# A mixture-of-experts trunk in fp32: the experts' down products cut into matmuls of 256 moving columns

## What is computed

```python
def swiglu(h, w_gate, w_up, w_down):
    return (jax.nn.silu(h @ w_gate) * (h @ w_up)) @ w_down

def moe_swiglu(h, w_router, w_gate, w_up, w_down):
    logits = (h @ w_router).astype(jnp.float32)
    top_vals, top_idx = lax.top_k(logits, TOP_K)          # TOP_K = 2 of 8
    gates = jax.nn.softmax(top_vals, axis=-1)
    comb = jnp.sum(jax.nn.one_hot(top_idx, N_EXPERTS, dtype=jnp.float32) * gates[..., None], axis=-2)
    out = jnp.zeros_like(h)
    for e in range(N_EXPERTS):
        out = out + comb[..., e:e + 1].astype(h.dtype) * swiglu(h, w_gate[e], w_up[e], w_down[e])
    return out
```

## Time and profile before

| | us |
|---|---|
| median of 3 runs | 1464.48 (1464.02 to 1464.84) |
| span of the profiled execution | 1463.9 |
| TensorE busy | 1434.9 |
| VectorE busy | 1167.5 |
| ScalarE busy | 925.6 |
| DMA queue of the weights, share of 16 engines | 77.5% |

### The profile page before, as it was taken

The page is one execution under the profiler, slowest core; times in us unless marked ns, Lnnn a source line. Parts: engine busy times, 40 slices in busy tenths (PEclk is TensorE's granted clock), DMA queues, the critical chain, the costliest instruction groups (busy, mean ns, idle before and its releaser), DMA issues.

```text
span 1463.9 us, 25480 instructions
## 1 busy us (share of the span) xinstructions
PE 1434.9 (98%) x10712; PEld 1312.7 (90%) x10712; DVE 1167.5 (80%) x1101; ACT 925.6 (63%) x918; POOL 42.5 (3%) x62
## 2 busy tenths in 40 slices
PE   7999999999999999999999999999999999999996
PEld 6899999998889889999999888999999898999994
DVE  6676556568637998998988998899798889989895
ACT  3845434444516777776776767676676767767675
POOL 2030000003020000000000000000000000000000
PEclk9999999999998999999999999999999999999998
DMA  8466555553219998999999999899999989999931
GB/s 332 144 227 227 189 189 199 199 184 136 72 49 417 368 382 336 366 363 339 357 348 368 332 378 360 335 357 353 351 349 361 367 342 354 357 350 360 355 146 45
DMA packets 60001, 426.14 MB, mean 291 GB/s; under 512 B 7025, under 2 KB 7153, under 8 KB 8689
## 3 DMA queue, kind: packets, MB, share of 16 engines
q1 hardware_dynamic: 58752, 422.60, 77.5%
q10 hardware_dynamic: 1136, 1.91, 0.4%
HBM read 423.44 MB, written 1.05 MB: 290 GB/s over the span
## 4 chain that ended last, share of the span: by engine, by line
PE 96%; ACT 1%; DVE 1%; POOL 1%; issue 1%; DMA 0%; ACTq 0%; SPq 0%; POOLq 0%; DVEq 0%
PE ps L1850 42%; PE ps L1872 21%; PE ps L1540 10%; PE ps L1563 5%; PE ps L1454 3%; PE ps L1838 2%; PE ps L1602 2%; PE ps L1486 2%; PE ps L1705 1%; PE ps L1857 1%; PE ps L1819 1%; PE ps L1649 1%; PE ps L1469 1%; POOL hn L1412 1%; PE ps L1677 0%
## 5 line engine op out<-in xcount | busy, mean ns | idle before, releaser
L1252 DVE TENSOR_TENSOR w_lo<-ring,w_hi 128x2048 fp32r<-128x2048 f32 x336 | 766.6, 2290 | 98.7 <-ACT w_hi L663 96.7
L663 ACT CAST w_hi<-ring 128x2048 fp32r<-128x2048 f32 x336 | 641.0, 1911 | 163.4 <-PE ps L1850 163.4
L1850 PE MATMUL ps<-w_hi,xg_hi 128*96 128x256 f32 x1792 | 248.6, 281 | 1.2 <-DVE xg_lo L1258 1.2
L1850 PE MATMUL ps<-w_hi,xg_lo 128*96 128x256 f32 x1792 | 241.8, 277 | 0.0
L1850 PE MATMUL ps<-w_lo,xg_hi 128*96 128x256 f32 x1792 | 241.6, 277 | 0.0
L1850 PEld LDWEIGHTS ps<-w_hi,xg_lo 128*96 128x96 f32 x1792 | 216.0, 161 | 0.0
L1850 PEld LDWEIGHTS ps<-w_lo,xg_hi 128*96 128x96 f32 x1792 | 215.7, 161 | 0.0
L1850 PEld LDWEIGHTS ps<-w_hi,xg_hi 128*96 128x96 f32 x1792 | 214.2, 162 | 1.3 <-DVE xg_lo L1258 1.3
L841 DVE TENSOR_TENSOR w_lo<-ring,w_hi 128x2048 fp32r<-128x2048 f32 x56 | 130.1, 2325 | 74.1 <-ACT w_hi L478 74.0
L478 ACT CAST w_hi<-ring 128x2048 fp32r<-128x2048 f32 x56 | 106.7, 1907 | 98.3 <-PE ps L1540 87.4
L1872 PE MATMUL ps<-w_lo,ht_hi 128*96 128x512 f32 x448 | 123.5, 397 | 0.2 <-DVE w_lo L1252 0.2
(11 more groups left out here) (286 smaller groups left out, 1376.4 us busy)
## 6 DMA issues: line engine op xcount, KB each, us to landing
ring<-in_moe_w_gate SPq DMA_DIRECT2D x112, 1024.0 KB, 6.8
ring<-in_moe_w_up SPq DMA_DIRECT2D x112, 1024.0 KB, 6.7
ring<-in_moe_w_down SPq DMA_DIRECT2D x112, 1024.0 KB, 6.8
ring<-in_ffn_w_gate SPq DMA_DIRECT2D x14, 1024.0 KB, 4.8
ring<-in_ffn_w_up SPq DMA_DIRECT2D x14, 1024.0 KB, 4.8
ring<-in_ffn_w_down SPq DMA_DIRECT2D x14, 1024.0 KB, 4.9
ring<-in_lru_w_in SPq DMA_DIRECT2D x7, 1024.0 KB, 12.4
ring<-in_attn_w_qkv SPq DMA_DIRECT2D x6, 1024.0 KB, 4.8
```

The costliest lines, as they stand in the source:

```text
L663: nc.scalar.copy(w_hi[:, (SPLITS + n) % PARTS], ring[:, s]).then_inc(hi_done, 1)
L1252: V.tensor_tensor(w_lo[:, part], ring[:, ORDER_MOE[n % SLOTS]], w_hi[:, part].bitcast(F32), ALU.subtract).then_inc(lo_done, 1)
L1850: mm = nc.tensor.matmul(ps[0:CAP, c % 2, m * CHF:(m + 1) * CHF], xs[a][:, k], w[b][:, k], start=(k == 0 and (a, b) == (0, 0)), stop=(k == ...
```

## The change

In the experts' down product each matmul of 512 moving columns becomes two of 256. The four matmuls of a half `f` have the same stationary block; they write half 0 and half 1 of bank 2, then half 0 and half 1 of bank 3. `start`, which marks the first write into a bank of a new sum, is given to the first half of each bank alone.

```diff
                     for f in range(2):
-                        for g in range(2):
-                            mm = nc.tensor.matmul(ps[0:CAP, 2 + g, :], hs[a][:, c % 2, f], w[b][:, f, g * 512:(g + 1) * 512],
-                                                  start=(c == 0 and f == 0 and (a, b) == (0, 0)),
-                                                  stop=(c == NCH - 1 and f == 1 and b == 1))
+                        for g in range(4):
+                            cols = slice((g % 2) * 256, (g % 2) * 256 + 256)
+                            mm = nc.tensor.matmul(ps[0:CAP, 2 + g // 2, cols], hs[a][:, c % 2, f], w[b][:, f, g * 256:(g + 1) * 256],
+                                                  start=(c == 0 and f == 0 and g % 2 == 0 and (a, b) == (0, 0)),
+                                                  stop=(c == NCH - 1 and f == 1 and b == 1), skip_group_check=True)
                 mm.then_inc(parts_used, 1)
```

## The result

| | before | after |
|---|---|---|
| median, us | 1464.66 (1464.02 to 1465.0) | 1475.46 (1475.16 to 1475.86) |
| span of the profiled execution | 1463.9 | 1473.6 |
| ratio, 95% interval | | 1.0076 (1.0062 to 1.009) |

The changed kernel is **0.76% slower**. The forecast was 0.4% faster, with a range that ended at 1469.5 us. The time is that of the fourth rival, the slow rhythm locked in, which was given 0.12 and 1476.2 us.

What follows compares the result with a forecast made beforehand. TensorE's own stream was taken as the bound; 73 quick rounds saving 0.08 us each give 5.8 us, so 1464.5 - 5.8 = 1458.7 us. Own range 1455 to 1461.5; 8 in 10: 1450.5 to 1469.5.

Steps and rivals of the forecast that it cites:

- fourth rival: Gate and up: slow stretches pass unchanged through short down products and transposes; all 73 quick rounds turned gives 1476.2 us; chance 0.12.
- the 2.66 us of lead: Down product: the low part it reads at 808.48 was finished 2.66 us early, so TensorE hardly waits.
- The reading of the mix: Gate and up: from their busy sum, about 39 of 112 blocks were taken as slow and 73 as quick.
- The new down product takes over the rhythm of what stands ahead of it: Down product: 2.72 us instead of 2.80 in quick rounds, 0.08 us less; 2.80 in slow rounds, nothing less.
- quick rounds: Rounds whose gate and up matmuls of 256 columns start 113.4 ns apart, against 116.7 in slow ones; 5.50 against 5.66 us.
- third rival: Down product: each short matmul at 118 ns makes it 2.83 us, 0.03 more; 1467.9 us in all; chance 0.08.
- 73 quick rounds: Expert rounds: this count, some ten either way, times 0.08 us saved per down product gives 5.8 us less.
- over 645: Sign in the gate and up busy sum: 640.75 us if the mix stays, over 645 if more blocks turned slow.
- The point from which it decides, 24 rounds: Fourth rival's break-even: with 24 quick rounds turned slow, 3.9 us gained meets 3.8 lost.
- The argument against rival 4: Before the change, quick rounds follow quick ones through the same transposes; this was held against the slow rhythm locking in.
- all quick (1449.3): First rival: the quick rhythm spreads to all gate-and-up blocks and down products, 15.2 us less; chance 0.17, in whole or by half.
- The rule of the Trainium skill: Each isolated matmul costs about 2.5 ns extra; the 1344 added ones would cost 3.4 us, giving 1467.9 us.

Runs made afterwards that it cites:

- k_same: Changed kernel with both halves f of one destination directly after each other, the same 24 matmuls; 1466.76 us, ratio 1.0010 to the kernel before.
- k_two: Kernel before with down passes 1 and 2 at 256 columns, pass 3 at 512, equal destinations in pass 3 from chunk 9 to 12; 1459.06 us, ratio 0.9963.
- k_two_b: As k_two, but chunk 13 has equal destinations in passes 1 and 2 and a long third pass; 1466.36 us, ratio 1.0011 to the kernel before.
- x1: Changed kernel with another down-product form in each expert; expert 0 does one transpose more per round: rounds of 8.43 us against the changed kernel's 8.62.

## Why the prediction was wrong

- **What bounds the kernel: right.** TensorE's stream alone, before and after; waits, clock and the 2.66 us of lead played no part.
- **The reading of the mix: right in its number, loose in its working.** (5.56 - 5.50) / 0.16 is 0.375 and not 0.35, which is 42 slow and 70 quick blocks. Counted block by block, the timeline of the kernel before has the 73 quick ones that the text used.
- **The new down product takes over the rhythm of what stands ahead of it: right.** 2.72 us in quick rounds, as forecast. In slow rounds it takes 2.83 instead of 2.80: a slow stretch with alternating destinations runs at the 118 ns of the earlier trace rows, not the 116.7 of the earlier trace rows. That is the size of the third rival, in slow rounds alone. With equal destinations (k_same) it is 2.80.
- **The term that failed is the count: 73 quick rounds.** It was read off the kernel before and carried over, with "some ten either way" for its shift and no reason for either. The text itself says that "what is decisive in those rows is the rhythm at which a stretch is entered". That was the reason not to carry the count over: the change alters what stands ahead of each entry. There are 14 quick rounds now, and the sign that the text had named for this came, a busy sum of gate and up of 650.45 us where "over 645" meant that more had turned slow. By the forecast's own prices: 59 rounds turned at 0.16 us is 9.4, 98 slow down products at 0.03 is 2.9, 14 quick ones at 0.08 give back 1.1: 11.2 us, where the windows of the expert phase grew by 11.6 (983.35 to 994.93) and the median by 10.8. The profiled span grew by 9.7, since its expert phase began 2.1 us earlier (450.04 against 452.14). Nothing ahead of that point was changed, and in the other runs it lies anywhere from 448.8 to 452.6 us.
- **Rival 4 named the outcome and the price, and only half its mechanism.** It said that a slow stretch passes through a down product of short matmuls unchanged. It does, in the first expert from the start on. But the quick rhythm doesn't pass through: behind the quick round at 829.49 the next gate is slow, every time in that kernel. The point from which it decides, 24 rounds, was passed by far.
- **The argument against rival 4 was weak.** "Quick rounds follow quick ones through the same transposes" is only in part true of the kernel before, and a long product stands between there, so it said nothing of a short one. In seven of its eight experts the quick round of chunk 7 is followed by two rounds at the slow rhythm, with no scatter or gather between. TensorE's timeline of the kernel before, gate passes of chunk 7 and of chunk 8 in expert 1, 0.91 and 0.93 us apart:

```profile
631.42 1.07 PE L1850 MATMUL ps<-w_hi,xg_lo 128*96 128x256 f32 x8
632.33 1.07 PE L1850 MATMUL ps<-w_lo,xg_hi 128*96 128x256 f32 x8
...
639.86 1.10 PE L1850 MATMUL ps<-w_hi,xg_lo 128*96 128x256 f32 x8
640.79 1.10 PE L1850 MATMUL ps<-w_lo,xg_hi 128*96 128x256 f32 x8
```

So the trace already showed that a round's rhythm doesn't follow from the round ahead alone. Each chance for a count that nothing in the profile bounds should have been wide; between all quick (1449.3) and all slow (1476.2) the range had to hold both ends.
- **The rule of the Trainium skill** ("TensorE: Matmul & The Clock Gate", section "Back-to-back issue gap"), a fixed price for each isolated matmul, had the right sign, and that was luck: the estimate by it was 3.4 us, and the kernel lost 10.8. Its mechanism isn't what the runs show: with one and the same number of short matmuls the kernel takes 1475.5 or 1466.8 us, by order alone, and in quick rounds the split product is the shorter one (2.72 against 2.80 us).

What sets the two rhythms is **open**. The traces show that they exist, that a stretch keeps one of them, and that the pattern repeats to 0.01 us from one expert to the next where both have the same form and the same state at their start. The runs show that instructions between two stretches redraw it, in a way that neither length, count, destination nor the last pass explains by itself, that one down product changes ten rounds behind it, and that the same instructions can enter either pattern (k_two and k_two_b, expert 0). So what is shown is where the 10.8 us went; why the new order turns 59 rounds slow is not. No run here separates the memory for the moving columns, the weight loads, PSUM or the timing of the other engines as the cause.

## What to carry to other kernels

Where TensorE's stream is the bound, read matmuls from start to start, shape by shape, and look whether one shape has more than one rhythm; if it has, the count of each is a term of any forecast and doesn't survive a change of what stands ahead. A form can be chosen by trying several in one run, one per repetition of the loop, but confirm it as a whole kernel and over several executions: what one repetition leaves behind can decide the next, and the first one can start in either pattern. A split that makes the parts cheaper than the whole in one stretch (226.8 against 233 ns here) may be worth its gain only in some of its passes: cutting two passes of three gave 0.28%, and cutting all three cost 0.76%.

## What the runs showed of the hardware

- Matmuls of 256 moving fp32r columns run at 113.4 or at 116.7 ns (118 where the destination alternates), with weight loads of 96 or 128 columns beside them; matmuls of 512 take 233 ns in either case.
- One transpose more in a round made it 0.2 us shorter in some rounds (8.42 against 8.62 us, x1's expert 0 and, at 8.43, k_extra's chunks 8 to 10) and 0.06 us longer in others (8.68, k_extra's chunk 7).
- The same instructions, from the start of the program on, took 124.21 us in one execution and 127.05 in another (expert 0 of k_two and k_two_b).
- The order of 24 equal matmuls moved the kernel by 0.6% (1466.8 against 1475.5 us), and one down product of 14 moved the next expert by 2.4 us (123.82 against 126.24).
